# At most four gathers of expert rows under way on GpSimd, in a kernel of two transformer blocks

## What is computed

```python
q = (xb @ w_q).reshape(PEER_BLOCK, PEER_HEADS, 2, PEER_HALF)          # 8 heads, 2 halves of 128
s = jnp.einsum('thjd,hjkd->thjk', q, sub_keys)
sv, si = lax.top_k(s, PEER_TOPK)                                      # 16 of 128 keys for each half
...
eidx = i1 * PEER_N_KEYS + i2                                          # 16 of 16384 experts, per head and token
g = jax.nn.softmax(cs, axis=-1)
u = expert_u[eidx]                                                    # rows of 1024 fp32
v = expert_v[eidx]
act = jax.nn.gelu(jnp.einsum('td,thkd->thk', xb, u), approximate=False)
return jnp.einsum('thk,thkd->td', (g * act).astype(v.dtype), v)
```

## Time and profile before

| | us |
|---|---|
| median of 3 runs | 2808.6 |
| lowest and highest | 2806.57, 2818.02 |
| span of the profiled execution | 3036.1 |

### The profile page before, as it was taken

The page is one execution under the profiler, slowest core; times in us unless marked ns, Lnnn a source line. Parts: engine busy times, 40 slices in busy tenths (PEclk is TensorE's granted clock), DMA queues, the critical chain, the costliest instruction groups (busy, mean ns, idle before and its releaser), DMA issues. The chain is left out here.

```text
span 3036.1 us, 28172 instructions
## 1 busy us (share of the span) xinstructions
PE 2390.3 (79%) x9768; PEld 1675.2 (55%) x9768; DVE 1750.3 (58%) x3620; ACT 574.3 (19%) x1560; POOL 1201.9 (40%) x1058
## 2 busy tenths in 40 slices
PE   6998899889756865998686953874887824999988
PEld 5847788565644544885452732442764312556755
DVE  3305410278997886476777768768777695000510
ACT  3411300112322120000112102411132000112321
POOL 0000000005887676375554775765666572000000
PEclk9998999999977986999898876887968956999999
DMA  3321234338999999699977997988998996342366
GB/s 144 139 107 60 80 141 155 132 129 338 414 367 350 355 366 413 260 418 414 358 268 287 349 411 294 350 329 352 415 381 334 384 409 260 111 161 101 150 232 246
DMA packets 173228, 832.05 MB, mean 274 GB/s; under 512 B 20880, under 2 KB 21136, under 8 KB 156192
## 3 DMA queue, kind: packets, MB, share of 16 engines
q0 software_dynamic: 147456, 536.94, 46.3%
q1 hardware_dynamic: 25632, 293.33, 24.6%
HBM read 828.09 MB, written 2.10 MB: 273 GB/s over the span
## 5 line engine op out<-in xcount | busy, mean ns | idle before, releaser
L1192 POOL DMA_INDIRECT expert_rows<-in_peer_u,chosen x512 | 656.4, 1282 | 1035.2 <-DVE chosen L1763 673.0
L1192 POOL DMA_INDIRECT expert_rows<-in_peer_v,chosen x512 | 542.1, 1059 | 294.3 <-issue 147.1
L1266 DVE SCALAR_TENSOR_TENSOR expert_rows<-expert_rows,u 128x1024 f32<-128x1024 f32 x512 | 603.7, 1223 | 64.4 <-DMA expert_rows<-in_peer_u,chosen 36.6
L2905 PE MATMUL mlp_up<-mlp_xT,mlp_slab 128*128 128x384 f32 (+1 forms) x1024 | 243.7, 395 | 100.9 <-issue 63.9
L1226 PE MATMUL expert_sum<-expert_rows,expert_diag 128*128 128x512 f32 x496 | 241.6, 633 | 37.3 <-ACT expert_diag L1213 28.2
L2905 PEld LDWEIGHTS mlp_up<-mlp_xT,mlp_slab 128*128 128x128 f32 x1024 | 161.5, 198 | 188.4 <-issue 91.4
L1276 DVE SCALAR_TENSOR_TENSOR h<-expert_rows,expert_coef,h 128x1024 f32<-128x1024 f32 x194 | 251.3, 1295 | 14.0 <-DMA expert_rows<-in_peer_v,chosen 9.0
L1276 DVE SCALAR_TENSOR_TENSOR u<-expert_rows,expert_coef,u 128x1024 f32<-128x1024 f32 x190 | 246.2, 1296 | 14.1 <-DMA expert_rows<-in_peer_v,chosen 12.0
L691 PE MATMUL product<-uT,in_slab 128*128 128x272 f32 (+1 forms) x1024 | 238.3, 388 | 8.1 <-DMA in_slab<-in_w_in 8.1
L2896 PE MATMUL mlp_down<-mlp_slab,upT 128*128 128x512 f32 x512 | 226.0, 597 | 12.4 <-issue 12.4
L691 PEld LDWEIGHTS product<-uT,in_slab 128*128 128x128 f32 x1024 | 192.2, 192 | 39.8 <-issue 8.7
(11 more groups left out here) (543 smaller groups left out, 3225.2 us busy)
## 6 DMA issues: line engine op xcount, KB each, us to landing
in_slab<-in_w_in SPq DMA_DIRECT2D x34, 2048.0 KB, 7.6
mix_slab<-in_w_in SPq DMA_DIRECT2D x16, 2048.0 KB, 8.3
mlp_slab<-in_w_up SPq DMA_DIRECT2D x16, 2048.0 KB, 8.3
mlp_slab<-in_w_down SPq DMA_DIRECT2D x16, 2048.0 KB, 7.6
expert_rows<-in_w_in SPq DMA_DIRECT2D x9, 2048.0 KB, 7.7
mix_slab<-in_ssd_w_out SPq DMA_DIRECT2D x8, 2048.0 KB, 8.4
out_slab<-in_w_out SPq DMA_DIRECT2D x6, 2048.0 KB, 8.1
mix_slab<-in_sc_w_out SPq DMA_DIRECT2D x4, 2048.0 KB, 8.6
```

Source lines behind the costliest of these rows:

```text
L1192: pool.indirect_dma_start(out=self.row(n), out_offset=None, in_=self.tables[0 if dot else 1], in_offset=bass.IndirectOffsetOnAxis(ap=picks ...
L1266: dve.scalar_tensor_tensor(self.row(n), self.row(n), 1.0, u, ALU.mult, ALU.mult, accum_out=dot).then_inc(self.rows_used, 1)
L2905: ins = pe.matmul(bank[n % UPS][:, 0:W], slab[i % R][:, k, j * P:(j + 1) * P], xT[:, k, :], start=k == 0, stop=k == KD - 1)
```

## The change

When POOL issues gather n, it first waits, beside the wait for its place, until gather n-4 has landed. The semaphore it reads is that of the earlier gather's place; no other engine's program changes.

```diff
     RING = 16
+    COMING = 4
     DIAGS = 6
...
                 elif before >= 0:
                     pool.wait_ge(self.rows_used, self.by_vector(before + 1))
+                earlier = n - self.COMING
+                if earlier >= 0:
+                    pool.wait_ge(self.landed[earlier % self.RING], 16 * (earlier // self.RING + 1))
                 pool.indirect_dma_start(
                     out=self.row(n), out_offset=None, in_=self.tables[0 if dot else 1],
```

## The result

The changed kernel takes 3094.02 us (median of 4, 3090.80 to 3098.45) against 2808.93 of the kernel before on the same chip: ratio 1.1009, interval 1.0991 to 1.1027, so 285 us slower. The forecast was 2836. Its sign was right, its size a tenth of what came.

The account below looks back on a forecast made before the run. The prediction saw no single bound: DMA nearly full, PE and DVE alternately full, gathers binding only where DVE had used up the ring. Slower gathers, summed by stretch after cover, added 27 us to 2808.6, giving 2836; range 2798 to 2880.

Parts of the forecast that it names:

- (a): The added wait instruction on POOL: when already satisfied it costs 0 us, up to 20 us if not hidden.
- (b): At POOL's gathers: more than four are under way, so the wait bites; traffic ran 17 us past the last issue.
- (d): Beside a 2 MB weight slab: POOL stands with four allowed, so the backlog that later fills the DMA engines is never made.
- slower than I say: Rival, chance 0.15: blocked gathers beside weight slabs cost a whole slab's worth each, giving 2878 us (2858 to 2890).
- step (c): POOL's gather loop with four under way: 5.1 to 6.1 us, taken as 1.43 us a gather, 0.15 above full rate.
- 1000 to 1100: Stretch in us of the earlier profile: 70 gathers, already at 1.43 us each with about four under way, so 0 us added.
- upper bound of 68 us: Added time over the listed profile stretches if nothing is covered by other work; the lower bound was 0.
- The cover: Gather delays hidden by landed rows or busy PE; in the MLP, over 200 us of matmuls left, so 0 us added.
- a cushion: Argument for the no-change rival, chance 0.24: DVE's dots wait only 36.6 us for gathers, so landed rows absorb delays.
- The stalls: PE's stops where gathers alone fill the DMA engines: 175 of 227.5 us, taken as belonging to the profiled execution only.
- faster: Rival, chance 0.11: PE's stalls under a deep backlog are partly in ordinary executions; four ends them, saving 50 us: 2786.
- The profiled span: Sign in the profile after: the span, 3036.1 us before, may well fall, since its stalls need a deep backlog.

Follow-up runs that it names:

- c16: The changed kernel with the limit `COMING` set to 16 instead of 4, so the added wait is always satisfied: 2808.6 us, ratio 0.9992 to the kernel before.
- scan4: The changed kernel with its limit of four narrowed to gathers 128 to 255, beside the stage `scan`: 2846.8 us, ratio 1.0145 to the kernel before.
- project4: The changed kernel with its limit of four narrowed to gathers 0 to 127, beside the stage `project`: 2848.2 us, ratio 1.0133 to the kernel before.
- c3: The changed kernel with `COMING` set to 3 instead of 4: 3447.1 us, one execution, where the kernel before took 3005.5.
- swap4: The changed kernel with POOL's two waits in the other order, so the gather itself carries the landing wait: 3071.9 us, ratio 1.0944 to the kernel before.
- mlp4: The changed kernel with its limit of four narrowed to gathers 853 to 1023, beside the MLP: 2858.3 us, ratio 1.0169 to the kernel before.
- rest4: The changed kernel with its limit of four narrowed to gathers 256 to 852: 3103.1 us, ratio 1.0318 to the kernel before at 3005.5.

## Why the prediction was right or wrong

Right: the sign. (a) the satisfied wait costs nothing: c16, 0.9992. (b) the limit bites: POOL waits for landings 256 times, and after the last issue at 2787.5 traffic ends at 2792.5, 5 us and not 17. PE waits 67.5 us for `adt` instead of 55.5 in c16. (d) as a direction only: with four, the slab stretches run at 324 to 351 GB/s instead of 369 to 413; but 128 gathers cost as much beside no slab (scan4, 37 us) as beside eight (project4, 38), so the slabs are not where the loss of `project` comes from, and the rival "slower than I say" is not borne out in its reason, though the time lay beyond its 2878.

Wrong, in four steps. Three of them multiply: 290 / 27, that is 11.

1. **The rate, step (c).** 1.43 us was taken, +0.15 to full rate. It is 1.67, +0.37 in `scan`: a factor of 2.5, and outside the range of 1.27 to 1.53. The range was read from a gather at three under way, 6.1 us, which is close to c3's loop of 6.1 to 6.2; but then 1.05 us of a slow issue was taken off, and the loop was divided by four as if it did not grow with the number under way. POOL's restart was set equal to DVE's 0.34, which was DVE's idle time and not its restart (0.02), and is 0.76; by swap4 that is worth little. And the check against 1000 to 1100 of the earlier trace rows went in a circle: that there were four under way in it was worked out from the loop that it was to confirm. The fit of the Trainium skill was held against the whole loop, 3.2 against 5.1 to 6.1 us, where it gives the part behind POOL's record (above).

2. **The count.** The sum went over the stretches of the earlier trace rows only. They hold 525 of the 1024 gathers, 455 without those counted at nothing in 1000 to 1100. Even its upper bound of 68 us was one for half the kernel; at its own 0.15 all gathers give 154. This is a factor of 2.25.

3. **The cover.** 27 of 68 us were let through, 40%. Measured: 290 of some 1024 x 0.37 = 379 (an estimate, since 0.37 is the price in `scan`), 77%, and 78% in scan4. Two views misled. The 36.6 us of DVE's waits for gathers in the earlier trace rows were read as a cushion, from a profile in which PE stood for some 175 us while the gathers went on. Without them c16 has

```profile
DVE expert_rows L1270 <- DMA expert_rows<-in_peer_u,chosen: 94.8, 50, 4.9
...
DVE u L1280 <- DMA expert_rows<-in_peer_v,chosen: 38.8, 29, 4.2
...
PE sums L1047 <- DVE adt L961: 55.5, 2, 46.8
```

and 36 us more for `h`, 170 us in all where the kernel before has 58; in the MLP alone it is 49 against 13. DVE already lived on the supply. And the MLP was said to hide its part because PE had over 200 us left; that was again PE delayed by its stall. The cover is 14 us, and the MLP costs 48 (mlp4) where 0 was forecast.

4. **The stalls.** "If they were in ordinary executions too, the median could not be 2808.6" joined a profile and a median that need not have been in the same state. Its number held, since the result came without the stalls on both sides; its cause did not. The rival "faster" named a mechanism that the runs bear out for the longest stall (a backlog beside which PE stops, and which a limit ends) and the condition under which it decides; at 2808 us there is no such stall to end, and at 3034 us eight gain 4%.

By stretch, the forecast against the difference of the stage in which it lies (c16 to the changed kernel): 720 to 920 12 and 27 (project4 38); 1000 to 1100 0 and 54; 1268 to 1405 3 and 55; 1700 to 1800 7 and 0; 1900 to 2000 3 and 48; 2100 to 2200 2 and 30; 2400 to 2500 0 and 52. The norm and the router, 17, were in no stretch. The largest misses, 45 to 54, have two reasons: in two the row had a rate below full (358 and 349 GB/s) and the price was set near zero for that, while `scan` runs at 397 to 401 GB/s in c16; in the other two PE was taken for a cover.

The profiled span did not fall: 3096.7 after 3036.1.

Left open: how the change itself stands where the kernel before takes over 3000 us (c3 and rest4 ran there, the full limit of four never did), what starts that state, what the router's 98 gathers cost at the usual level, and how much of the loop is the path to memory and how much the engines' packets, since no gather of another size was run.

## What to carry to other kernels

A limit on DMAs under way costs little while number x full-rate time exceeds the loop (six: 7.7 against 7.1 us, 1%; five: 6.4 against 7.0, 4%), and the loop must be measured at that number: it grows with the number (5.4 us for one, 7.1 for six). Before costing, make the stretches of the sum cover every instance of what is changed, and make sure that the profile is of the same state as the median; a stalled engine makes waits elsewhere look small and cover look large. Where a kernel has a second, slow level, a limit that is just not felt at the usual level (eight here, 1.0019) may be worth having: it gave 4.2% at the slow one, in two executions against three.

## What the hardware showed that was not expected

- A gather of 512 KB by GpSimd alone takes 5.4 us from issue to next issue, and with a limit of six the DMA engines are 1.01 busy, with five 0.94, though each gather needs only 1.28 us of them.
- GpSimd starts 0.76 us after a landing when the wait is an instruction of its own ahead of one that carries another wait, and 0.26 when the gather carries it. VectorE starts 0.02 us after a landing, also where a second wait stands beside that for the landing.
- In a second state, PE and ACT stand for tens of us, ACT up to 145, in stretches where gathers are queued, with the DMA engines at 1.01 to 1.03. With at most eight queued the longest of these is gone (464 to 334 us for the MLP), with four that of `project_two` too.
- One packet of the instruction queue q8 comes for about 250 instructions of PE and PEld, in a stall as outside it, so a hole in that queue tells of PE's pace and not of a late fetch.
